# A 31-tap depthwise convolution: from three engines and diagonal weights to column-quarter products on TensorE fed by shifted copies

## The reference, cut to what matters

```python
def conformer_conv(x, w_pw1, b_pw1, w_dw, b_dw, g, b, w_pw2, b_pw2):
    h = x @ w_pw1 + b_pw1
    a, gate = jnp.split(h, 2, axis=-1)
    h = a * jax.nn.sigmoid(gate)
    h = lax.conv_general_dilated(          # depthwise, causal, CONV_WIDTH = 31 taps
        h, w_dw[:, None, :].astype(h.dtype), window_strides=(1,),
        padding=[(CONV_WIDTH - 1, 0)],
        dimension_numbers=("NWC", "WIO", "NWC"),
        feature_group_count=D_MODEL) + b_dw
    h = jax.nn.silu(layer_norm(h, g, b))
    return h @ w_pw2 + b_pw2
...
x = layer_norm(ALPHA * x + mix, ln_mix_g[l], ln_mix_b[l])
ffn = grouped_moe(x, router_w, router_bias, moe_w_gate[l], moe_w_up[l], moe_w_down[l])
```

## Time and profile before

| | |
|---|---|
| median of 3 runs | 1563.94 us (1562.49 to 1570.64) |
| profiled execution: its time, its span | 1561.53 us, 1559.8 us |
| PE busy, share of the span | 1399.9 us, 90% |
| VectorE, ScalarE, POOL busy | 428.5, 272.6, 61.5 us |
| moved by DMA | 307.75 MB, mean 197 GB/s |
| mean granted clock of TensorE | 0.939 |

### The profile page before, as it was taken

The page is one execution under the profiler, slowest core; times in us unless marked ns, Lnnn a source line. Parts: engine busy times, 40 slices in busy tenths (PEclk is TensorE's granted clock), DMA queues, the critical chain, the costliest instruction groups (busy, mean ns, idle before and its releaser), DMA issues.

```text
span 1559.8 us, 15911 instructions
## 1 busy us (share of the span) xinstructions
PE 1399.9 (90%) x6338; PEld 903.6 (58%) x6338; DVE 428.5 (27%) x961; ACT 272.6 (17%) x598; POOL 61.5 (4%) x97
## 2 busy tenths in 40 slices
PE   7868689999979996869999997999889996999997
PEld 6654444454435774445444535876667685888743
DVE  1992311111130232221111103145522304222201
ACT  4022110010010333111000112131143403000000
POOL 4910000000000000000000000000000000000000
PEclk9979789999989995879999998998999998999999
DMA  9710259999995051329999995131223033344420
GB/s 361 230 48 18 96 201 395 396 393 393 393 393 176 0 179 65 108 74 393 393 395 396 393 393 202 54 109 54 76 86 108 1 108 108 109 161 162 162 81 27
DMA packets 146506, 307.75 MB, mean 197 GB/s; under 512 B 5634, under 2 KB 29950, under 8 KB 146447
## 3 DMA queue, kind: packets, MB, share of 16 engines
q1 hardware_dynamic: 139968, 298.85, 52.4%
q10 hardware_dynamic: 6479, 8.07, 1.6%
HBM read 305.86 MB, written 1.06 MB: 197 GB/s over the span
## 4 chain that ended last, share of the span: by engine, by line
PE 81%; DVE 11%; DMA 5%; issue 2%; ACT 1%; ACTq 0%; DVEq 0%; POOL 0%; POOLq 0%
PE psum L233 35%; PE psum L1289 13%; PE psum L1325 6%; PE psum L544 6%; PE psum L2512 5%; DMA ring<-in_moe_w_up 5%; DVE arena L878 3%; PE psum L1336 3%; PE psum L759 2%; PE psum L733 2%; PE psum L1310 2%; PE psum L425 1%; PE psum L1474 1%; PE psum L1472 1%; PE psum L2170 1%
## 5 line engine op out<-in xcount | busy, mean ns | idle before, releaser
L233 PE MATMUL psum<-xT,ring 128*128 128x256 f32 (+2 forms) x1792 | 405.4, 388 | 6.2 <-POOLq L405 5.2
L233 PEld LDWEIGHTS psum<-xT,ring 128*128 128x128 f32 x1792 | 341.4, 192 | 66.5 <-issue 11.0
L1289 PE MATMUL psum<-ring,arena 128*64 128x512 f32 x1024 | 226.2, 594 | 3.2 <-issue 1.7
L1289 PEld LDWEIGHTS psum<-ring,arena 128*64 128x64 f32 x1024 | 73.9, 137 | 138.5 <-issue 138.2
L1325 PE MATMUL psum<-ring,arena 128*64 128x512 f32 x512 | 117.7, 614 | 1.8 <-ACT arena L1250 1.8
L233 PE MATMUL psum<-arena,x_nat 128*128 128x128 f32 x512 | 69.1, 292 | 16.7 <-issue 16.7
L233 PEld LDWEIGHTS psum<-arena,x_nat 128*128 128x128 f32 x512 | 63.5, 202 | 29.1 <-issue 28.2
L1325 PEld LDWEIGHTS psum<-ring,arena 128*64 128x64 f32 x512 | 36.9, 141 | 70.5 <-issue 68.8
L1180 DVE TENSOR_TENSOR arena<-psum,arena 64x512 f32<-64x512 f32 x32 | 22.3, 695 | 200.1 <-ACT arena L1236 200.1
L2512 PE MATMUL psum<-ring,arena 128*128 128x512 f32 x176 | 75.7, 592 | 0.0
L878 DVE SCALAR_TENSOR_TENSOR arena<-arena,vec 128x256 f32<-128x256 f32 x150 | 75.0, 575 | 0.7
(11 more groups left out here) (302 smaller groups left out, 1308.5 us busy)
## 6 DMA issues: line engine op xcount, KB each, us to landing
ring<-in_moe_w_gate SPq DMA_DIRECT2D x32, 2048.0 KB, 15.8
ring<-in_moe_w_up SPq DMA_DIRECT2D x32, 2048.0 KB, 19.7
ring<-in_moe_w_down SPq DMA_DIRECT2D x32, 2048.0 KB, 15.7
ring<-in_w_in SPq DMA_DIRECT2D x11, 2048.0 KB, 15.3
ring<-in_w_up SPq DMA_DIRECT2D x22, 1024.0 KB, 7.7
ring<-in_a_w_pw SPq DMA_DIRECT2D x6, 2048.0 KB, 19.5
ring<-in_w_down SPq DMA_DIRECT2D x5, 2048.0 KB, 7.7
ring<-in_w_kv SPq DMA_DIRECT2D x4, 2048.0 KB, 19.4
```

The costliest lines, as they stand in the source:

```text
L233: last = nc.tensor.matmul(dst, lhsT, rhs, start=(n == 0), stop=(n == len(pairs) - 1))
L1289: last = pe.matmul(bank(j)[part, :], tokens[:, k, side * SEATS:side * SEATS + SEATS], slot_k(u + n)[:, k, :], start=(k == 0), stop=(k == K ...
```

## The change

All eight chunks get their taps from PE. A product now holds four taps of 32 channels: the stationary block is 128x32 (partition 32j + i is tap 4q + j of channel i, and `quad_diag` has a one where i equals the column), and the moving operand holds, on its four groups of 32 partitions, the same 32 channels shifted by 0, 1, 2 and 3 tokens. Eight such products (`QUADS`) give 32 tap places, of which 31 are used; the four groups of 32 channels of a chunk write the four column quarters of one bank. POOL makes the blocks of one chunk in one multiplication. The shifted copies come through memory: ScalarE writes a chunk of `glu` to `glu_scratch` (`send`), and reads it back four times, each into 32 partitions (`fetch_shifted`), three buffers deep. `CONV_ORDER` lays the products of chunk n + 2 between the taps of chunks. Each chunk's result is read out with its bias; the first four are summed to give a shift (`shift_b`) that is subtracted from every chunk, and the sums of values and squares are added up chunk by chunk, so that variance is mean square less squared mean. The tap weights arrive in 8 DMAs of another layout instead of 2. The bias of the second projection is folded into ALPHA * x on VectorE. The 14 inputs at n == 3 stay there, with b_pw2 now spread over 128 partitions (512 KB instead of 4 KB).

```diff
+CONV_ORDER = [("glu", 0), ("glu", 1), ("glu", 2), ("taps", 0), ("glu", 3), ("taps", 1), ("glu", 4), ("taps", 2),
+              ("glu", 5), ("taps", 3), ("glu", 6), ("taps", 4), ("glu", 7), ("taps", 5), ("taps", 6), ("taps", 7)]
...
+            w_dw = a["a_w_dw"][0]
+            for q in range(QUADS):
+                taps = min(4, TAPS - 4 * q)
+                act.dma_start(rows[32 * (q % 4):32 * (q % 4) + 32, 2 + q // 4, 0:32 * taps].rearrange("p (j i) -> p j i", j=taps),
+                              w_dw[4 * q:4 * q + taps].rearrange("j (c i) -> c j i", i=32)).then_inc(consts_loaded, 16)
...
+            def taps(c):
+                j = conv_job("taps", c)
+                take_bank(j)
+                pe.wait_ge(shifted_loaded[c % REP_BUFS], 64 * (c // REP_BUFS + 1))
+                pe.wait_ge(blocks_made, c + 1)
+                for q in range(QUADS):
+                    for g in range(CONV_GROUPS):
+                        last = pe.matmul(bank(j)[32 * g:32 * g + 32, 0:SEQ], blocks[:, c % BLOCK_BUFS, q, g, :],
+                                         shifted[:, c % REP_BUFS, g, 4 * q:4 * q + SEQ], start=(q == 0),
+                                         stop=(q == QUADS - 1))
+                last.then_inc(job_done, 1)
...
+            for c in range(KC):
...
+                pool.tensor_tensor(blocks[:, c % BLOCK_BUFS, :, :, :], diag, cols.unsqueeze(3).broadcast_to(shape),
+                                   ALU.mult).then_inc(blocks_made, 1)
...
+            def send(n):
+                act.wait_ge(glu_ready, n + 1)
+                act.dma_start(glu_scratch[n], glu[:, n % GLU_BUFS, :]).then_inc(glu_written[n % 2], 16)
+
+            def fetch_shifted(n):
+                act.wait_ge(glu_written[n % 2], 16 * (n // 2 + 1))
+                if n >= REP_BUFS:
+                    job_ready(act, conv_job("taps", n - REP_BUFS))
+                for tap in range(4):
+                    src = bass.AP(glu_scratch.tensor, n * P * WIDE + tap,
+                                  [[WIDE, 32], [32 * WIDE, CONV_GROUPS], [1, WIDE - 4]])
+                    act.dma_start(shifted[32 * tap:32 * tap + 32, n % REP_BUFS, :, :], src).then_inc(shifted_loaded[n % REP_BUFS], 16)
...
+                if 3 <= n < 3 + HALF:
+                    taps_out(n - 3)
+                send(n)
+                if n:
+                    fetch_shifted(n - 1)
                 if n == 3:
...
-                    act.dma_start(b_pw2, a["a_b_pw2"]).then_inc(inputs_loaded, 16)
+                    act.dma_start(b_pw2, a["a_b_pw2"][0].partition_broadcast(P)).then_inc(inputs_loaded, 16)
...
+            fetch_shifted(KC - 1)
+            for c in range(KC):
+                squares_of(c)
...
+            for c in range(1, KC):
+                dve_step(dve.tensor_tensor(conv[:, c, :], conv[:, c, :], mean_b, ALU.subtract))
+                dve.tensor_tensor(conv[:, c, :], conv[:, c, :], rstd_b, ALU.mult).then_inc(conv_normed, 1)
```

More of the change, by code:

```diff
@@ L567, in turned_in, with add_residual @@
                 bank_free[(first + c) % BANKS], 1)
[L569 removed]
+    def add_residual(first, tiles=(1, 2), scaled=False):
         j = first
@@ L575, in add_residual @@
                 xs = x_nat[:, t, half * 512:half * 512 + 512]
-                ins = nc.vector.scalar_tensor_tensor(xs, xs, ALPHA, bank(j), ALU.mult, ALU.add)
+                if scaled:
+                    ins = nc.vector.tensor_tensor(xs, xs, bank(j), ALU.add)
+                else:
+                    ins = nc.vector.scalar_tensor_tensor(xs, xs, ALPHA, bank(j), ALU.mult, ALU.add)
                 ins.then_inc(bank_free[j % BANKS], 1)
@@ L612, in _ @@
             pool_step(pool.memset(by_distance, MASKED))
+            pool_step(pool.tensor_copy(quad_diag, ident[:, 0:32]))
+            for part in range(1, 4):
+                pool_step(pool.tensor_tensor(quad_diag, quad_diag, ident[:, 32 * part:32 * part + 32], ALU.add))
             pool_step(pool.memset(upto[:, :], 1.0))
@@ L669, in _ @@
             last.then_inc(job_done, 1)
[L672 to L701, removed]
+    GLU_BUFS, REP_BUFS, BLOCK_BUFS, WIDE = 4, 3, 3, PAD + SEQ + 2
+    HALF = KC // 2
+    glu = carve(0, GLU_BUFS, WIDE)
+    sig = carve(1152, 2, SEQ)
+    squares = carve(1664, 3, SEQ)
+    conv = carve(2432, KC, SEQ)
+    blocks = carve(4480, BLOCK_BUFS, QUADS, CONV_GROUPS, 32)
+    shifted = carve(9900, REP_BUFS, CONV_GROUPS, WIDE - 4)
+    shift_b, mean_b, rstd_b = carve(13310, SEQ), carve(13566, SEQ), carve(13822, SEQ)
+    mean_sq = carve(14078, SEQ)
+    sig_ready, glu_ready = sem("sig_ready"), sem("glu_ready")
+    glu_written = [sem(f"glu_written{i}") for i in range(2)]
+    shifted_loaded = [sem(f"shifted_loaded{i}") for i in range(REP_BUFS)]
+    blocks_made, conv_out = sem("blocks_made"), sem("conv_out")
+    shift_summed, centred, squared, squares_used = (
+        sem("shift_summed"), sem("centred"), sem("squared"), sem("squares_used"))
+    moments_ready, conv_normed, act_ready = sem("moments_ready"), sem("conv_normed"), sem("conv_activated")
+    SHIFT_BANK, MEAN_BANK, SQUARE_BANK = BANKS, BANKS + 1, BANKS + 2
     @stage
@@ L724, in _ @@
             products(bank(FJ["relb"])[0:HEADS, 0:3 * P], [(rel_w[:, :], buckets)]).then_inc(job_done, 1)
[L726 to L748, removed]
+            mean_part(6)
+            square_part(6)
+            mean_part(7)
+            square_part(7)
             j = FJ["pw2"]
@@ L765, in _ @@
         def _(pool):
[L766 to L781, removed]
+            for c in range(KC):
+                if c >= BLOCK_BUFS:
+                    job_ready(pool, conv_job("taps", c - BLOCK_BUFS))
+                shape = [P, QUADS, CONV_GROUPS, 32]
+                diag = quad_diag.unsqueeze(1).unsqueeze(1).broadcast_to(shape)
+                cols = tap_cols[:, :, CONV_GROUPS * c:CONV_GROUPS * c + CONV_GROUPS]
+                pool.tensor_tensor(blocks[:, c % BLOCK_BUFS, :, :, :], diag, cols.unsqueeze(3).broadcast_to(shape),
+                                   ALU.mult).then_inc(blocks_made, 1)
@@ new lines, in taps_out, with squares_of @@
+            def taps_out(c):
+                j = conv_job("taps", c)
+                job_ready(act, j)
+                act.activation(conv[:, c, :], bank(j)[:, 0:SEQ], ACT.Identity, bias=column("a_b_dw", c)).then_inc(
+                    bank_free[j % BANKS], 1)
+                act.wait_ge(bank_free[j % BANKS], j // BANKS + 1)
+                act.nop().then_inc(conv_out, 1)
+            def squares_of(c):
+                act.wait_ge(centred, c + 1)
+                if c >= 3:
+                    act.wait_ge(squares_used, c - 2)
+                act.activation(squares[:, c % 3, :], conv[:, c, :], ACT.Square).then_inc(squared, 1)
@@ L818, in _ @@
             act.dma_start(rel_scratch, by_distance).then_inc(rel_written, 16)
[L820 to L843, removed]
         @block.vector
@@ L901, in _, with taps_out @@
-            add_residual(FJ["pw2"])
+            def taps_out(c):
+                j = conv_job("taps", c)
+                job_ready(dve, j)
+                dve.scalar_tensor_tensor(conv[:, c, :], bank(j)[:, 0:SEQ], column("a_b_dw", c), shift_b, ALU.add,
+                                         ALU.subtract).then_inc(centred, 1)
+                dve.wait_ge(centred, c + 1)
+                dve.nop().then_inc(bank_free[j % BANKS], 1)
+            for n in range(KC - 1):
+                gated(n)
@@ new lines, in _ @@
+            dve.wait_ge(inputs_loaded, INPUT_DMAS * 16)
+            for t in (1, 2):
+                dve_step(dve.scalar_tensor_tensor(x_nat[:, t, :], x_nat[:, t, :], ALPHA, b_pw2, ALU.mult, ALU.add))
+            dve.wait_ge(shift_summed, 1)
+            dve_step(dve.tensor_scalar(shift_b, psum[:, SHIFT_BANK, 0:SEQ], 1.0 / (HALF * P), None, ALU.mult))
+            for c in range(HALF):
+                dve.tensor_tensor(conv[:, c, :], conv[:, c, :], shift_b, ALU.subtract).then_inc(centred, 1)
```

130 lines of the change are left out of this document (71 added, 59 removed).

## The result

The changed kernel takes 1569.79 us in the median of 20 runs, the kernel before 1564.55 us in as many: a ratio of 1.0029, 95% interval 1.0017 to 1.0041 (here and below the ratio is worked out over all runs, so it is not quite the quotient of the two medians). It is slower by 0.3%, where a gain of 10 us was forecast and 1567 was the upper end of the range.

What follows compares the result with a forecast made beforehand. Convolution taps, on the path to the second projection's end, were taken as the bound. A gain of 24.1 us less 14.2 in payments left 9.9, stated as 1554 us, eight in ten from 1543 to 1567.

Steps and rivals of the forecast that it cites:

- The bound: Convolution taps limit the kernel; a microsecond won before the second projection's end at 168.6 counts fully, nothing elsewhere.
- The sum without waits: From stage start through second projection, PE never waiting: end at 144.5 us against 168.6, a gain of 24.1.
- rival 4: PE taps: column quarters do not hide loads of differing weights; 7.0 us a chunk, a loss of 15, 1579 us; 6%.
- The rule that the prediction cites: PE weight loads overlap running products only when row groups differ; taps would take 10.4 us a chunk, 52 us more.
- rival 5: POOL's making of tap blocks takes above 10.9 us a chunk; at 14 us, 25 us more; 2%.
- What must be paid out of that: Costs before the second projection's end: constants, three waits for copies, clock; 14.2 us of the 24.1 gain.
- The landing of the copies: PE waits of 2 us before first taps, 3.2 before chunk 3's taps, 4.0 before the first square.
- The clock: PE slower after idling: 1.8 us for the third wait, 1.0 for the second, 2.8 together.
- The first three chunks: First projection on PE: 96 records are three chunks in 21.10 us, so 7.03 a chunk and 56.3 for eight.
- Rival 3: ScalarE's queue of DMA issues binds every chunk; some 12 us more, 1563 to 1566 us, no change; 20%.
- Rival 1: The shifted copies hide; only constants and some 3 us of waits remain, gain 18, 1546 us; 27%.

Runs made afterwards that it cites:

- experiment 1: Changed kernel with SyncE's loads of units 6 to 9 (gate and up weights) held until chunk 7's taps: 1551.44 us against 1567.09 for the kernel before.
- experiment 5: Changed kernel with only units 6 and 7 held, until chunk 3's taps: 1559.55 us against 1564.1 for the kernel before.
- experiment 7: As experiment 1, and unit 4 waits for chunk 0's taps, unit 5 for chunk 1's: 1550.8 us against 1564.1 for the kernel before.
- experiment 3: Changed kernel with SyncE released to load unit 1 before the eight tap-weight DMAs: 1571.5 us, ratio 1.0019 to the kernel before.
- experiment 2: Changed kernel with the 14 input DMAs issued by SyncE behind unit 5 instead of ScalarE: 1563.07 us against 1567.09 for the kernel before.
- experiment 8: Changed kernel with the edits of experiment 7 and experiment 2 together: 1545.22 us against 1563.9 for the kernel before.
- experiment 6: Control: the kernel before, with loads of units 6 to 9 held until the sum over channels: 1563.12 us against 1564.1 unedited.
- experiment 4: Changed kernel without copies through memory, all taps reading one buffer filled once with 0.5: 1541.15 us against 1567.09 for the kernel before.

## Why the prediction was wrong

The bound was right. What is won or lost before the end of the second projection goes through one for one: 173.35 less 168.6 is 4.7, the first experts 5.4, the medians 5.2; and in experiment 1 that end moved by 18.2 and the profiled execution by 18.0. The profiled execution is 8.6 longer than that of before; the 3 us beyond come in later stages whose code is unchanged, and the medians do not have them.

The sum without waits was right within 2 us, and too high: 16.36 for the start (16.4 forecast), taps 3.59 us a chunk in place of 3.84, 5.0 from the last sum to the second projection (4.9), 29.7 for that (30.0). The four column quarters overlap with different weights as they did in the earlier trace rows, so rival 4 fell: 64 loads of 106 to 110 ns, 7 us if laid end to end, lie inside 3.59 us. The rule that the prediction cites from the Trainium skill, "TensorE: Matmul & The Clock Gate", part 3, is not borne out by this trace either. (The 53 ns in the sum made by that rule would be 60 by the prediction's own 0.234 ns a column; nothing hangs on it.) POOL's blocks took 1.9 us each, so rival 5 fell too.

What failed is the part "What must be paid out of that", in its terms for the waits and for the clock, and one figure of the sum on PE.

- **The landing of the copies.** I took 6.5 us from the earlier trace rows for the first and 2.5 for chunk 3's, as if no ring load ran by then. Measured were up to 9.4 and 4.0 to 4.7, and for chunk 2, for which I had no wait at all, 9.0. I had written that SyncE starts 4 MB "at this very moment" for chunk 7, and counted 4 us for its write where 6.49 came; at chunk 3 the same release stood in the code, and in the trace of before at 42.20, and I did not put it beside the fetch. Waits forecast: 2 + 3.2 + 4.0. Measured: 5.47 + 3.17 + 2.88 + 6.26 + 0.65, that is 18.4 in place of 9.2. Experiments 1 and 5 show that the loads are the cause: hold them, and 9.0 becomes 3.0. Experiment 7 shows it for the first wait. That the wait before the taps of chunk 3 came out near its forecast (2.88 for 3.2) is luck: from the end of that chunk's projection they began after 29.2 us, not 25.0, and the wait stayed short only because PE had lost 4.9 us at the taps of chunk 2 meanwhile.
- **The clock.** 2.8 us forecast. Only two of the waits were charged for it. Behind all of them the granted clock was at its lower level of 1.2 GHz for a time (0.50 from 45 to 47, 73.5 to 75.2, 86.85 to 88.8 and 121.2 to 126.8 us), and taps took 5.32, 5.35, 5.00 and 4.80 instead of 3.59, the first squares 2.93 instead of the 1.56 of experiment 1: 7.5 us. It is not a fixed price of a wait: in experiment 3, behind waits of 3.33 and 3.40 us, the clock stayed at 1.00 and taps took 3.66.
- **The first three chunks** of the projection took 23.42 in place of 21.10. The sum took over the figure of the kernel before. Experiment 3 clears unit 1's later load of it. Why they were slow stays open, below.

9.2, 4.7 and 2.3 more, less 2.0 on taps: 14.2, and the forecast end, 144.5 + 14.2 = 158.7, plus these 14.2 more is 172.9 against 173.35.

Rival 3, "ScalarE's queue binds every chunk", named blocked issues and a time of 1563 to 1566, the nearest of all. Its mechanism was half right: the issues were blocked (router_b alone 4.44 us), but not by ScalarE's own traffic. With the ring quiet the inputs went out in 7.3 us, and with them still in front no middle wait was left (experiments 1 and 5). In the change itself their place in the order did cost something, about the 4.3 us of experiment 2, as long as the loads blocked them. It did so again in 7 against 8: a wait of 3.55 us in the traces, and 5.6 us by the medians, with intervals of 5 us each way. Rival 1 gave 1546 for copies that hide; experiment 8 has it, 1545.22, but only with the edits of 7 and 2, which the change lacks.

## What to carry to other kernels

When small transfers come onto the critical path, look up what else the semaphore that releases them releases: a large prefetch set free by the same job delays them, though it comes from another queue (8.1 to 10.1 us beside it, 2.8 to 3.4 without it). Where in the chip they meet, these runs do not show. Price a small DMA by its landing beside such loads, not by its size, and count the slower products behind an idle stretch with it. Loads that are not needed for long can be held by one wait on a later job; here that turned 0.3% slower into 1.0% faster, and with paced loads and inputs moved off the queue into 1.2%.

## What the runs showed of the hardware

- The same four copies of 142 KB landed after 2.8 to 3.4 us with the ring quiet and after 8.1 to 10.1 us beside two 2 MB loads issued 1 to 4 us earlier on another queue; a write of 144 KB after 1.8 us (experiment 1) and 6.5 us (the change).
- A DMA issue on ScalarE's queue takes about 0.45 us, but can stand for 4 to 6 us while 2 MB loads from SyncE run (4.44 in the change, 4.35 in experiment 7, 5.66 in the earlier trace rows, and 5.98 in experiment 4, where no copies were made). The block of 14 took 6.7 and 7.3 us with these loads held (experiments 6 and 1), 13.6 and 17.2 us beside them (the kernel before, the change).
- Column quarters of 128x32 fp32 weights and 256 columns run at 56 ns a record (3.59 us for 64), a quarter of the 220 ns that a full-width record takes in the earlier trace rows; so four of them take the time of one such record.
- The first three chunks of the projection took either 20.96 us (runs 1 and 2, started at 15.6 to 15.8 us) or 22.6 to 23.7 (the change and the others). The kernel before took 21.10. Where they took longer, the first 6 us ran at about half pace. These are, in this order, the changed kernel, run 1 and experiment 4 (columns: PE busy with its records, PEclk, DMA share, GB/s):

```profile
16.00:18.00 2.00, 1.64 (x4) 1.00 1.05 388
18.00:20.00 2.00, 2.00 (x6) 1.00 1.06 390
```

```profile
16.00:18.00 2.00, 2.00 (x10) 1.00 1.05 387
18.00:20.00 2.00, 2.00 (x11) 1.00 1.08 401
```

```profile
16.00:18.00 2.00, 2.00 (x6) 0.60 1.06 389
18.00:20.00 2.00, 2.00 (x6) 0.55 1.06 392
```

  In the change the granted clock reads 1.00 all through. But experiment 4 has the same pace, 6 records in 2 us where 11 are usual, beside a granted clock of 0.60 and 0.55, and the DMA columns are alike in all three. That points to the clock, missed by its record in the change and its like, and not to the loads. It is not shown: no run was made to tell these apart, and the cause stays open.
